# Differential attention in a two-block model: the order of the query-block rounds within each head

## The chip, the cores and the metric

One core of one Trainium2 chip. The metric is the device time of one execution in microseconds (us). The whole program (two model blocks) is timed, and the change touches one stage of it, the attention.

## The reference

512 tokens, model width 1024. A first block (convolutions, spatial gating, an expert lookup) is followed by a second one: a state-space mixer, a feed-forward part, then differential attention and another feed-forward part. The attention is what matters here:

```python
def block(args):                                   # one block of 128 queries
    idx, qc = args
    rel = k_pos[None, :] - q_pos[:, None]
    bias = rel_bias[t5_causal_bucket(rel)]...
    s = jnp.einsum("bqhcd,bkhcd->bhcqk", qc, k) * scale      # c: two halves of a head
    s = jnp.where(rel <= 0, s + bias, NEG_INF)
    pm = jax.nn.softmax(s, axis=-1)
    attn = pm[:, :, 0] - lam * pm[:, :, 1]
    return jnp.einsum("bhqk,bkhe->bqhe", attn, v)
...
o = rms_norm(o, subln) * (1.0 - lam_init)
return o.reshape(...) @ w_o
```

There are 8 heads and 4 blocks of 128 queries. A block sees only the keys up to its own end, so block 0 has 128 keys, block 1 has 256, block 2 has 384 and block 3 has 512.

## The kernel before

Each engine has its own instruction stream, written out by hand; semaphores tie them together. The attention works through `QUERIES = HEADS * NR = 24` rounds, three for each head. `ROUNDS` (L351) says which query blocks a round holds: blocks 0 and 1 together (128 and 256 columns side by side in a bank), then block 2 (384 columns), then block 3 (512 columns). Below they are called the **narrow pair**, the **third** and the **widest**. `members(v)` lists the blocks of round v; `exps_until(v)` gives the count of exponentials that are finished when round v is, which other engines wait for.

A round v passes through these steps:

- TensorE, `scores2(v)` (L1118): the products of queries and keys for both halves, into two of four score banks (`score_bank`). It waits for the exponentials of round v-2, which free the banks.
- VectorE, `highest(v)`: per row the extreme of the scores, over the far keys a plain reduction (L2595), over the last 256 keys together with the bias (L2598). The narrow pair needs no L2595, but twice the L2598.
- ScalarE, `exps(v)` (L1734): the exponentials with their sums, per block one for each half.
- VectorE, `share(v)` (L2608, L2610) and `blend(v)` (L2618): the ratio of the two softmaxes' sums, and their weighted difference.
- TensorE, `turn(v)` (L1131): transposes of that difference, one for each 128 keys.
- ScalarE, `turned(v)` (L1744): copies them to where the next product reads them.

When all rounds of a head are through, TensorE does `values(h)` (L1143), the product with the values. ScalarE takes it out in `head_out(h)` (L1751, L1754). `head_stat`, `spread` (L1155, L1170), `batch_root` (L1760, two table loads beside it), `batch_inverse` (L2624) and `head_norm` (L2631) normalise finished heads in between; POOL makes the low half of a finished head in `norm_low` (L2722), and splits weights for the output product (L2675, L2677 before the rounds, L2750, L2752 beside them).

The loops are staggered by hand. VectorE does `highest(u+1)`, now and then `head_norm`, then `share(u)`, `blend(u)`. TensorE does `scores2(u+2)`, `turn(u-1)`, and after it, by the place j of round u-1 in its head, `values(h-1)` (j = 0) or `head_stat(h-1)` (j = 1). ScalarE does `exps(u+1)`, `turned(u-1)`, and `head_out(h-1)` if round u-1 has j = 0. `scores2(0)` and `scores2(1)` are issued earlier, inside the products that make the second half of the values (L1088); ScalarE copies those values out (L1715) between `exps(1)` and `exps(2)`, and `scores2(3)` waits for these copies. `values(4)` and others wait for `on_ready`, the signal of `head_norm` (`SPREADS_BEFORE`), since they share a bank.

Of the kernel before, what the change touches and what calls it, by code (L numbers as in the profile page):

```python
# [17 lines left out]
NT = SEQ // P  # L18
# [54 lines left out]
def build(nc, A, first=0, last=99):  # L73
# [24 lines left out]
    with ctx:  # L98
# [28 lines left out]
        def view(arena, at, *shape):  # L127
            n = int(np.prod(shape))
            v = arena[:, at:at + n]
            if len(shape) == 2:  # L130
                v = v.rearrange("p (a b) -> p a b", b=shape[1])
            elif len(shape) == 3:
                v = v.rearrange("p (a b c) -> p a b c", b=shape[1], c=shape[2])
            elif len(shape) == 4:
                v = v.rearrange("p (a b c d) -> p a b c d", b=shape[1], c=shape[2], d=shape[3])
            return v
# [211 lines left out]
        qgain = R[:, 14008:14009]  # L348
        ROWS16 = 4 * NT
        sel = view(R, 14016, ROWS16, ROWS16)  # L350
        ROUNDS = ((0, 1), (2,), (3,))  # L351
        NR = len(ROUNDS)
        BATCHES = ((0, 1, 2), (3, 4), (5, 6, 7))
        BATCH = [g for g in range(3) for h in BATCHES[g]]
# [34 lines left out]
        def members(v):  # L389

            at = 0
            for part, qt in enumerate(ROUNDS[v % NR]):
                w = (qt + 1) * P
# [2 lines left out]

        def exps_until(v):

            return 2 * (v // NR * NT + ROUNDS[v % NR][-1]) + 2

        def score_bank(u):

# [133 lines left out]
        def _(pe):  # L536
# [505 lines left out]
            if stage("attn"):  # L1042
# [59 lines left out]
                def scores2(v):  # L1102

                    h = v // NR
                    if v % NR == 0:
                        pe.wait_ge(kq_ready, HEADS + h + 1)
                    if v == 0:
                        pe.wait_ge(evac_done, used(TILE0["w_v"] + 3))
                    if v == 1:
                        pe.wait_ge(gq_sqrt, 2 * HEADS)  # L1110
                    if v >= 2:
                        pe.wait_ge(exp_done, exps_until(v - 2))
                    if v == 3:
                        pe.wait_ge(evac_done, used(TILE0["w_v"] + 7))
                    for part, u, qt, at, w in members(v):
                        for c in range(2):
                            rows, out = slice(c * HD, (c + 1) * HD), banks[score_bank(v) + c]
                            mm = pe.matmul(out[:, at:at + w], KQ[rows, HEADS + h, qt * P:(qt + 1) * P], KQ[rows, h, 0:w],  # L1118
                                           start=True, stop=True)
                    mm.then_inc(at_sc, 1)  # L1120

                def turn(v):

                    pe.wait_ge(cb_done, v + 1)
                    if v == 0:
                        pe.wait_ge(exp_done, exps_until(1))
                    if v >= 2:
                        pe.wait_ge(tr_ev, exps_until(v - 2) // 2)
                    for part, u, qt, at, w in members(v):
                        for kt in range(qt + 1):  # L1130
                            mm = pe.transpose(banks[4 + v % 2][:, at + kt * P:at + (kt + 1) * P],  # L1131
                                              att[:, v % 2, at + kt * P:at + (kt + 1) * P], ident)
                    mm.then_inc(tr_mm, 1)
# [657 lines left out]
        def _(ve):  # L1791
# [764 lines left out]
            if stage("attn"):  # L2556
# [47 lines left out]
                def share(v):  # L2604
                    n, u = len(ROUNDS[v % NR]), v // NR * NT + ROUNDS[v % NR][0]
                    r = ratio[:, v % 2, 0:n]
                    ve.wait_ge(exp_done, exps_until(v))
                    ve.reciprocal(r, sums[:, u:u + n, 1])  # L2608
                    ve.drain()
                    ve.scalar_tensor_tensor(r, r, nlam, sums[:, u:u + n, 0], ALU.mult, ALU.mult)  # L2610
                    ve.drain()
# [338 lines left out]
```

## Time and profile before

| | |
|---|---|
| median of 3 runs | 2934.83 us (2932.98 to 2935.81) |
| profiled execution: its own time | 2934.74 us |
| profiled execution: span of the trace | 2932.9 us |
| busy over the span: TensorE, VectorE, POOL, ScalarE | 2622.4, 1937.4, 1673.5, 826.2 us |
| attention rounds, first L2598 to last L2618 | 2391.65 to 2472.23 us |
| in the stretch 2384 to 2480 us: VectorE, TensorE, ScalarE busy | 74.88, 79.22, 64.22 us of 96 |
| mean granted TensorE clock in that stretch | 0.91 of full |

The profile gives busy times by engine and line, what ended each idle time, and the instructions in order of time. A stretch can be queried alone, which is what a change of one stage asks for: the rounds take 80.6 of 2932.9 us.

### The profile page before, as it was taken

The numbers are of one execution on the slowest core, as the hardware profiler recorded it, in microseconds if no ns is written. First come the engines' busy times: TensorE is split into PE (matmuls) and PEld (weight loads), VectorE is DVE, ScalarE is ACT, GpSimd is POOL, SyncE is SP. The second block draws the span as 40 slices with busy tenths as digits, with TensorE's granted clock in tenths as the row PEclk, the third lists the DMA queues.
The fourth block names the chain that finished last, engine by engine and source line by source line (L and its number), as shares of the span: only waits on it lengthen the run. The fifth ranks groups of instructions, "written<-read, shape, count | busy, mean of one in ns | idle before, by whom it ended". The sixth has DMA issues, their size and how long they took to land.

```text
span 2932.9 us, 32353 instructions
## 1 busy us (share of the span) xinstructions
PE 2622.4 (89%) x9810; PEld 1211.8 (41%) x9810; DVE 1937.4 (66%) x3944; ACT 826.2 (28%) x1800; POOL 1673.5 (57%) x1024
## 2 busy tenths in 40 slices
PE   7989888887888888887878999999999998999999
PEld 3454333333333333333333684444444445444444
DVE  7947777777777777777877683666336596566523
ACT  2422222222222222222234461222112246222101
POOL 5544444444444444444535877777776651677776
PEclk9999999999999999999999979999999999999999
DMA  4259999999999999999972322333322320233332
GB/s 138 71 192 421 421 421 417 411 420 417 413 416 409 417 410 421 411 411 419 414 312 69 105 74 88 94 101 105 117 95 86 117 72 8 79 100 102 120 98 82
DMA packets 133100, 696.18 MB, mean 237 GB/s; under 512 B 29867, under 2 KB 31180, under 8 KB 67052
## 3 DMA queue, kind: packets, MB, share of 16 engines
q0 software_dynamic: 73728, 536.90, 44.4%
q1 hardware_dynamic: 59244, 157.74, 16.6%
q8 instruction: 60, 0.98, 0.1%
q14 instruction: 68, 0.56, 0.1%
HBM read 686.72 MB, written 7.86 MB: 237 GB/s over the span
## 4 chain that ended last, share of the span: by engine, by line
PE 33%; DMA 26%; POOLq 16%; DVE 12%; issue 7%; ACT 3%; DVEq 2%; POOL 2%; ACTq 0%; SPq 0%
DMA R<-expert_uv_dram,idx 25%; PE bank L573 20%; PE bank L787 8%; POOLq L2678 8%; POOLq L2676 7%; DVE R L2106 3%; DVE Z L2128 1%; POOL R L2703 1%; DVE xt L2391 1%; ACT Z L1390 1%; DVE R L1851 1%; PE bank L1143 1%; PE bank L956 1%; DVE ci L2052 0%; DVE R L2118 0%
## 5 line engine op out<-in xcount | busy, mean ns | idle before, releaser
L787 PE MATMUL bank<-R,Z 128*128 128x512 f32 x2048 | 972.5, 619 | 227.2 <-ACT Z L1390 222.3
L2703 POOL DMA_INDIRECT R<-expert_uv_dram,idx x512 | 595.2, 1162 | 722.7 <-PE bank L787 673.2
L573 PE MATMUL bank<-R 128*128 128x512 f16 (+1 forms) x3936 | 865.6, 381 | 8.9 <-DVE R L1835 6.1
L2106 DVE SCALAR_TENSOR_TENSOR R<-R 128x1024 f32<-128x1024 f32 x512 | 622.9, 1222 | 198.2 <-DMA R<-expert_uv_dram,idx 196.8
L787 PEld LDWEIGHTS bank<-R,Z 128*128 128x128 f32 x2048 | 382.4, 195 | 800.4 <-issue 419.9
L2675 POOL TENSOR_TENSOR R<-wring,beat 128x1024 f16<-128x1024 f32 (+2 forms) x219 | 447.1, 2041 | 396.7 <-PE bank L573 349.2
L573 PEld LDWEIGHTS bank<-R 128*128 128x128 f16 (+1 forms) x3936 | 382.6, 98 | 490.3 <-issue 26.6
L2677 POOL TENSOR_TENSOR R<-wring,R 128x1024 bf16<-128x1024 f32 (+2 forms) x219 | 510.1, 2329 | 31.8 <-issue 0.3
L1390 ACT ACTIVATE Z<-consts,R 128x128 f32<-128x128 f32 x512 | 177.7, 394 | 322.1 <-DVE R L2118 320.0
L573 PE MATMUL bank<-Z,R 128*128 128x512 f16 x1104 | 239.9, 379 | 1.5 <-POOLq L2678 1.5
L1383 ACT ACTIVATE R<-R 128x2 f32<-128x2 f32 x256 | 52.1, 203 | 607.3 <-DVEq L2108 607.0
L573 PEld LDWEIGHTS bank<-Z,R 128*128 128x128 f16 x1104 | 107.8, 98 | 132.2 <-POOLq L2678 2.5
L1508 ACT ACTIVATE R<-bank,cols 128x512 f32<-128x512 f32 x88 | 68.4, 777 | 324.8 <-DVE bank L2361 324.8
L1879 DVE TENSOR_TENSOR hT<-hT,bank 128x512 f32<-128x512 f32 x32 | 22.0, 688 | 204.1 <-PE bank L573 204.1
L2361 DVE TENSOR_TENSOR bank<-bank,sq 128x512 f32<-128x512 f32 x88 | 61.2, 695 | 129.6 <-PE bank L573 124.7
L573 PE MATMUL bank<-aT,R 128*128 128x512 f16 (+1 forms) x576 | 130.7, 388 | 5.1 <-DVE aT L2170 4.4
L1267 ACT ACTIVATE bank<-hT 128x512 f32<-128x512 f32 x56 | 33.5, 598 | 246.9 <-DVE hT L1879 216.5
L2118 DVE SCALAR_TENSOR_TENSOR R<-R 128x2 f32<-128x2 f32 x256 | 56.2, 220 | 58.8 <-ACT R L1383 47.4
L573 PEld LDWEIGHTS bank<-aT,R 128*128 128x128 f16 (+1 forms) x576 | 56.9, 99 | 76.8 <-issue 8.2
L1851 DVE SCALAR_TENSOR_TENSOR R<-hT,cols,R 128x512 bf16<-128x512 f32 x48 | 82.5, 1732 | 0.7
L2367 DVE SCALAR_TENSOR_TENSOR R<-bank,cols,R 128x511 f32<-128x511 f32 x88 | 65.6, 745 | 16.7 <-issue 16.7
L806 PE MATMUL bank<-aT,Z 128*128 128x512 f32 x144 | 73.6, 592 | 0.0
(365 smaller groups left out, 2513.2 us busy)
## 6 DMA issues: line engine op xcount, KB each, us to landing
wring<-up_dram SPq DMA_DIRECT2D x88, 512.0 KB, 3.5
wring<-down_dram SPq DMA_DIRECT2D x32, 704.0 KB, 4.1
wring<-ple_dram SPq DMA_DIRECT2D x16, 640.0 KB, 3.9
wring<-w_in_dram SPq DMA_DIRECT2D x18, 512.0 KB, 3.5
R<-expert_uv_dram,idx POOLq DMA_INDIRECT x512, 12.2
wring<-glu_dram SPq DMA_DIRECT2D x16, 512.0 KB, 4.1
Z<-w_q_dram SPq DMA_DIRECT2D x11, 512.0 KB, 7.8
wring<-ple_a_dram SPq DMA_DIRECT2D x8, 640.0 KB, 5.9
```

The lines of the kernel that those rows point to most:

```text
L573: mm = pe.matmul(bank[:, :], low(w) if i else w, low(v) if j else v, start=(start and c == 0 and p == 0), stop=(stop and c == n - 1 and p ...
L787: mm = pe.matmul(banks[2 * par + c][:, :], diag[:, k % 4, :], pairs[:, slot, 1, c * SEQ:(c + 1) * SEQ], start=(k == 0), stop=(k == TOPK - 1))
L806: mm = pe.matmul(banks[6 + half][:, :], w[:, k * P:(k + 1) * P], aT[:, k, :], start=(k == 0), stop=(k == KT - 1))
L1390: ac.activation(diag[:, k % 4, :], ident, ACT.Copy, scale=actg[:, par, k:k + 1])\
L1508: ac.activation(conv[:, u, gv, :], banks[(2 * u + gv) % NBANK][:, :], ACT.Identity, bias=cols[:, bass.ds(at + b, 1)], scale=cols[:, bass.d ...
L1851: ve.scalar_tensor_tensor(low(parts[:, k, 1, :]), hT[:, k, :], col(gain, k), parts[:, k, 0, :], ALU.mult, ALU.subtract).then_inc(gn_ready, 1)
L2106: dot = ve.scalar_tensor_tensor(pairs[:, slot, 0, :], pairs[:, slot, 0, :], 1.0, ntok[:, T, :], ALU.mult, ALU.mult, accum_out=act[:, par, ...
L2675: po.tensor_tensor(wsp[:, slot, 0, 0:w], src, one.broadcast_to([P, w]), ALU.mult)
L2676: po.drain()
L2677: po.tensor_tensor(low(wsp[:, slot, 1, 0:w]), src, wsp[:, slot, 0, 0:w], ALU.subtract)
L2678: po.drain().then_inc(split_done, 1)
L2703: po.indirect_dma_start(pairs[:, slot, :, :].rearrange("p a b -> p (a b)"), None, A["expert_uv"], bass.IndirectOffsetOnAxis(idx[:, n % 2, ...
```

## The change

Within each head the widest round comes first, then the third, then the narrow pair. `exps_until` counts the exponentials over the rounds as they now stand.

```diff
-        ROUNDS = ((0, 1), (2,), (3,))
+        ROUNDS = ((3,), (2,), (0, 1))
...
         def exps_until(v):
 
-            return 2 * (v // NR * NT + ROUNDS[v % NR][-1]) + 2
+            return 2 * (v // NR * NT + sum(len(r) for r in ROUNDS[:v % NR + 1]))
```

No instruction is added or taken away. POOL's and SyncE's streams stay as they are. Below, `bank<-Z 128x512 x2` at L1118 are the scores of the widest round, 128x384 those of the third, 128x128 and 128x256 those of the narrow pair.

TensorE at the start of the attention rounds, where the value products (L1088) end; the difference, `-` before and `+` now:

```order
 L1088 MATMUL bank<-R 128x512 x12
+L1118 MATMUL bank<-Z 128x512 x2
+L1118 MATMUL bank<-Z 128x384 x2
+L1088 MATMUL bank<-R 128x512 x24
 L1118 MATMUL bank<-Z 128x128 x2
 L1118 MATMUL bank<-Z 128x256 x2
+L1118 MATMUL bank<-Z 128x512 x2
+L1131 MATMUL bank<-consts,R 128x128 x4
 L1118 MATMUL bank<-Z 128x384 x2
-L1088 MATMUL bank<-R 128x512 x24
-L1118 MATMUL bank<-Z 128x512 x2
```

The two score groups inside the value products are now the widest and the third, and the one that waits for the value copies (the second group behind the 24 products) is the widest instead of the narrow pair.

TensorE in the second head, around its first `values`, before:

```order
L1118 MATMUL bank<-Z 128x128 x2
L1118 MATMUL bank<-Z 128x256 x2
L1131 MATMUL bank<-consts,R 128x128 x3
L1143 MATMUL bank<-R 128x512
L1143 MATMUL bank<-R 128x384
L1143 MATMUL bank<-R 128x256
L1143 MATMUL bank<-R 128x128
L1118 MATMUL bank<-Z 128x384 x2
```

and now:

```order
L1118 MATMUL bank<-Z 128x512 x2
L1131 MATMUL bank<-consts,R 128x128 x4
L1143 MATMUL bank<-R 128x512
L1143 MATMUL bank<-R 128x384
L1143 MATMUL bank<-R 128x256
L1143 MATMUL bank<-R 128x128
L1118 MATMUL bank<-Z 128x384 x2
```

`values` and what stands behind it are where they were; ahead of it now stand the scores and the four transposes of a widest round, not those of a narrow pair.

VectorE at the end of the rounds, before:

```order
L2631 SCALAR_TENSOR_TENSOR xt<-aT,sub,bank 128x512
L2608 RECIPROCAL R<-R 128x1
L2610 SCALAR_TENSOR_TENSOR R<-R 128x1
L2618 SCALAR_TENSOR_TENSOR R<-Z,R 128x384
L2608 RECIPROCAL R<-R 128x1
L2610 SCALAR_TENSOR_TENSOR R<-R 128x1
L2618 SCALAR_TENSOR_TENSOR R<-Z,R 128x512
L2624 RECIPROCAL rstd<-rstd 16x128
```

and now:

```order
L2631 SCALAR_TENSOR_TENSOR xt<-aT,sub,bank 128x512
L2608 RECIPROCAL R<-R 128x1
L2610 SCALAR_TENSOR_TENSOR R<-R 128x1
L2618 SCALAR_TENSOR_TENSOR R<-Z,R 128x384
L2608 RECIPROCAL R<-R 128x2
L2610 SCALAR_TENSOR_TENSOR R<-R 128x2
L2618 SCALAR_TENSOR_TENSOR R<-Z,R 128x128
L2618 SCALAR_TENSOR_TENSOR R<-Z,R 128x256
L2624 RECIPROCAL rstd<-rstd 16x128
```

The last difference that VectorE forms is that of the narrow pair, in two instructions, instead of the widest block's in one.

## Rows read from the trace of the kernel before

**Rows 1.** The page, part 1: busy time, share of the span, instructions of each engine.

```profile
PE 2622.4 (89%) x9810; PEld 1211.8 (41%) x9810; DVE 1937.4 (66%) x3944; ACT 826.2 (28%) x1800; POOL 1673.5 (57%) x1024
```

**Rows 2.** Waits, 2384 to 2480 us: who waited for whom, us in total, times, longest.

```profile
DVE xt L2631 <- PE bank L1170: 2.4, 3, 1.3
DVE R L2595 <- PE bank L1118: 1.2, 1, 1.2
...
DVE R L2608 <- ACT Z L1734: 0.2, 1, 0.2
```

**Rows 3.** Timeline of VectorE, one head: start us, us, engine, line, operation.

```profile
2417.40 0.29 DVE L2598 CUSTOM_DVE_ANT_0 bank<-bank,R 128x128 f32<-128x128 f32 x1
...
2418.88 0.16 DVE L2608 RECIPROCAL R<-R 128x1 f32<-128x1 f32 x1
...
2420.08 0.42 DVE L2595 TENSOR_REDUCE R<-bank 128x2 f32<-128x256 f32 x1
...
2421.69 0.17 DVE L2608 RECIPROCAL R<-R 128x2 f32<-128x2 f32 x1
...
2422.89 0.68 DVE L2595 TENSOR_REDUCE R<-bank 128x2 f32<-128x512 f32 x1
...
2424.76 0.17 DVE L2608 RECIPROCAL R<-R 128x1 f32<-128x1 f32 x1
...
2425.83 0.29 DVE L2598 CUSTOM_DVE_ANT_0 bank<-bank,R 128x128 f32<-128x128 f32 x1
```

**Rows 4.** Timeline of ScalarE in the same head.

```profile
2416.28 0.69 ACT L1734 ACTIVATE Z<-bank,R 128x512 f32<-128x512 f32 x1 [1.37 <-DVEq L2602]
...
2417.53 0.20 ACT L1734 ACTIVATION_READ_ACCUMULATOR Z<-bank,R 128x1 f32 x1
...
2419.14 0.37 ACT L1734 ACTIVATE Z<-bank,R 128x128 f32<-128x128 f32 x1
...
2420.62 0.23 ACT L1734 ACTIVATION_READ_ACCUMULATOR Z<-bank,R 128x1 f32 x1
```

**Rows 5.** Timeline of TensorE in the same head.

```profile
2420.91 1.13 PE L1118 MATMUL bank<-Z 64*128 64x512 f32 x4 [0.48 <-ACT Z L1734]
2421.97 0.66 PE L1131 MATMUL bank<-consts,R 128*128 128x128 f32 x4
2423.02 0.93 PE L1118 MATMUL bank<-Z 64*128 64x128 f32 x8 [0.39 <-ACT Z L1734]
...
2424.26 2.32 PE L1143 MATMUL bank<-R 128*128 128x512 f32 x8
```

**Rows 6.** Timeline of all engines at the start of the rounds.

```profile
2389.05 2.38 POOL L2677 TENSOR_TENSOR R<-wring,R 128x1024 bf16<-128x1024 f32 x1
2389.63 1.82 DVE L2582 SCALAR_TENSOR_TENSOR R<-R 128x1 f32<-128x1 f32 x1 [0.18 <-issue]
...
2395.83 2.42 ACT L1715 ACTIVATE R<-bank,R 128x512 f32<-128x512 f32 x4
...
2398.40 1.65 PE L1118 MATMUL bank<-Z 64*128 64x128 f32 x8 [1.46 <-ACT R L1715]
...
2403.29 1.93 PE L1118 MATMUL bank<-Z 64*128 64x512 f32 x4
```

**Rows 7.** Timeline of VectorE, the three places where it waits in the rounds.

```profile
2440.94 0.75 DVE L2631 SCALAR_TENSOR_TENSOR xt<-aT,sub,bank 128x512 f32<-128x512 f32 x1 [0.92 <-PE bank L1170]
...
2450.88 0.42 DVE L2595 TENSOR_REDUCE R<-bank 128x2 f32<-128x256 f32 x1 [1.20 <-PE bank L1118]
...
2453.63 0.75 DVE L2631 SCALAR_TENSOR_TENSOR xt<-aT,sub,bank 128x512 f32<-128x512 f32 x1 [1.25 <-PE bank L1170]
```

**Rows 8.** Timeline of TensorE, an idle time without and two idle times with slow matmuls behind.

```profile
2433.95 0.93 PE L1118 MATMUL bank<-Z 64*128 64x128 f32 x8 [2.88 <-ACT Z L1734]
...
2445.90 4.09 PE L1143 MATMUL bank<-R 128*128 128x512 f32 x8 [0.94 <-DVEq L2632]
...
2469.94 4.02 PE L1143 MATMUL bank<-R 128*128 128x512 f32 x8 [1.87 <-DVEq L2632]
```

**Rows 9.** Busy time by stretch: stretch, length, PE, PEld, DVE, ACT, POOL, PEclk, DMA share, GB/s.

```profile
2445.90:2449.40 3.50, 3.50 (x6) 1.83 (x7) 3.08 (x14) 0.91 (x4) 0.00 (x0) 0.51 0.00 0
```

## The prediction, made before the changed kernel was run

> **What bounds the kernel now.** Begin with the busy times of the whole page [rows 1]: TensorE is busy 89% of the span, but that is a mean over sixteen stages, and the change touches only 80.6 us of the 2932.9. So the stage is read alone. Its list of waits [rows 2] shows who holds up whom: VectorE waits for TensorE's bank spreads 2.4 us in all, once 1.2 us for scores, and for exponentials 0.2 us. That is 3.8 us in 80.6; the other engines wait for VectorE far longer. The timeline of one head on VectorE [rows 3] shows why. From the start of one round's maxima to the start of the next step there are 1.48 us for the narrow pair (2417.40 to 2418.88), 1.61 for the third (2420.08 to 2421.69), 1.87 for the widest (2422.89 to 2424.76). Share and blend take 1.20 for the widest (2418.88 to 2420.08), 1.20 for the narrow pair (2421.69 to 2422.89) and 1.07 for the third (2424.76 to 2425.83). The six add up to 8.43 us, and that is just the head's period (2417.40 to 2425.83). VectorE never stands still in such a head: **it is the bound**, and a reordering doesn't change a sum. What can change are the start, the end, and the places where VectorE waits for others.
>
> **The change, part by part.**
>
> *Steady heads: nothing.* The cycle becomes widest, third, narrow pair. It stays at 8.43 us as long as the other two engines deliver in time. ScalarE: its exponentials take 1.45 us for the widest (2416.28 to 2417.73) and 1.71 for the narrow pair (2419.14 to 2420.85) [rows 4]. Between them lie the copy of the transposes and the two instructions that take a head out, 2.86 - 1.45 = 1.41 us. Before, the narrow exponentials ended at 2420.85 and their share began at 2421.69 [rows 3, 4]: 0.84 us of slack. Now the head's exit stands behind the narrow pair's exponentials and ahead of the widest's. Count from the end of the narrow maxima: ScalarE is free at 1.71 + 1.41 = 3.12; the widest maxima are ready at 1.07 + 1.87 = 2.94; the exponentials then end at 3.12 + 1.45 = 4.57, and their share is due at 2.94 + 1.20 + 1.61 = 5.75. That leaves 1.2 us, from which the values product may take some: ahead of it TensorE now has widest scores (1.13 us instead of 0.93) and four transposes (0.66 us, so at most 0.17 more than three; I take 0.12) [rows 5], 0.32 us in all. I keep 0.8 us of slack. TensorE: before, the widest scores ended at 2422.04 and were wanted at 2422.89 [rows 3, 5], 0.85 us; now they follow the exponentials of the third of the head before, and are wanted only after maxima of the narrow pair and a share, so the slack is no smaller. Nothing is added per head. At the two places where ScalarE loads tables for a square root, the exponentials ahead of the loads are now the widest's, 0.26 us shorter.
>
> *Start: +0.8 us.* Three small delays follow each other. The two score groups inside the value products are widest and third instead of narrow and third: +0.20 us on TensorE [rows 5]. POOL's weight split follows TensorE there, and VectorE's L2582 (1.82 us for one column) ends at 2391.45, just as POOL's L2677 ends at 2391.43 [rows 6]; so the first maxima start 0.20 later. Their widest form lasts 1.87 - 1.48 = 0.39 longer, but the second exponentials start only 0.32 later, since they waited 0.07 for the narrow ones before and now wait for their own maxima alone, and so do the value copies of 2.42 us behind them [rows 6]. The scores that wait for these copies are now the widest at the low clock, 1.93 instead of 1.65 us: +0.28 [rows 6]. Together 0.20 + 0.32 + 0.28 = 0.80. All of it is on the path, since VectorE takes these scores about as they come.
>
> *First bank spread (2440.94, VectorE waits 0.92) [rows 7]: +0.3 us.* VectorE arrives 0.39 later in its count of work, because the widest maxima precede. TensorE's chain to the spread starts from exponentials behind ScalarE's table loads: they come 0.39 + 0.2 later (0.39 the maxima; and 0.2 because ScalarE, free 2.86 - 2.55 = 0.3 us after the narrow maxima were ready [rows 3, 4], now waits for the longer TensorE chain as well), less 0.26; then the wider scores and the fourth transpose, +0.32. That is 0.65, against 0.39: 0.26 more waiting, rounded to 0.3.
>
> *Scores behind values of the fifth head (2450.88, waits 1.20) and the spread behind them (2453.63, waits 1.25) [rows 7]: -0.4 us.* The values product starts when VectorE has normed a head; all three maxima and the same shares lie before that point in either order, so it does not move. But VectorE now has widest maxima between this point and its wait, not after it: 0.39 us of work moves into the wait. The second wait keeps its length, as both sides hang on the same product.
>
> *End: -0.15 us.* The last round has three transposes instead of four (-0.12) and two short copies instead of a long one (a few hundredths).
>
> DMA issues, POOL's and SyncE's queues are not moved. Sum: 0.80 + 0.3 - 0.4 - 0.15 = **+0.55 us**. Behind the rounds TensorE runs the output product at once, so it passes on in full. Against the profiled execution's own time that is 2934.74 + 0.55 = 2935.3; the median of the runs lies 0.1 higher, so I say **2935.4 us**.
>
> **The clock, a term of the range.** Two values products took 4.09 and 4.02 us instead of 2.32 [rows 5, 8]; in the first the granted clock was 0.51 [rows 9], the lower of TensorE's two levels (1.2 GHz of 2.4). Ahead of them the engine had stood idle 0.94 and 1.87 us. Yet after 2.88 us idle at 2433.95 the scores still ran in 0.93 us [rows 8], so idle time alone does not tell where the clock falls. My sum leaves both slow products where they are, since the same instructions stand ahead of them. If neither were slow, 2 x 1.75 = 3.5 us go, and the start loses its 0.8: 0.55 - 4.3 = -3.8. If two more products are slow, +3.5: +4.1. The Trainium skill (TensorE: Matmul & The Clock Gate, What's actually happening) says that an engine left idle falls to the lower level and that the monitor runs freely, whatever the kernel does. By that rule the slow products could fall anywhere, and the time would move by those amounts without any cause in the order.
>
> **The rivals.**
>
> 1. *The low clock falls on other products* (0.25): 2931.0 to 2939.0, as worked out. For it: the idle times around the products shift by some tenths. Against: the waits that cause them stay.
> 2. *VectorE and POOL collide elsewhere* (0.09). L2582 shows such a collision: 1.82 us for one column. A POOL split lasts up to 2.38 us [rows 6], so one more or one less moves the time by at most that: 2933 to 2937.7. The Trainium skill (SBUF — State Buffer) calls the shared port pair an exclusive lock for a whole instruction; the end at 2391.45 beside POOL's 2391.43 agrees.
> 3. *Slower: the head's exit holds up the widest exponentials* (0.07). ScalarE runs in order, and behind the head's exit, which waits for the values product, now stand the exponentials that VectorE needs next, behind a longer TensorE chain. It decides once the product ends over 0.8 us later than I have it. At the low clock a product takes 1.75 us more; 1.75 - 0.8 = 0.95 us in each of 7 heads is 6.6, with the sum 2935.4 + 6.6 = 2942. For it: ScalarE's start is already late by some tenths. Against: the same exit stood ahead of the narrow exponentials with 0.84 us of slack, and no head showed a wait.
> 4. *Faster: the narrow pair last takes the waits away* (0.04). All three waits of rows 7 vanish (3.4), the last slow product runs at full clock (1.7) and L2582 no longer meets POOL (at most 1.8): 2934.8 - 6.9 = 2928. Against: two of the waits hang on a product that the change doesn't move.
>
> **How the numbers follow.** My forecast has the remaining 0.55: 2935.4, with the spread of the runs 2933.9 to 2936.9. The range takes in rivals 1 and 2: 2931.0 to 2939.0, and leaves out about 0.15 at both sides. 0.2% is 5.9 us, about what a measurement of this kernel can tell from no change; only rival 3 passes it upwards and rival 4 downwards. So faster 0.04, same 0.89, slower 0.07.
>
> **What would show it.** Right: a steady head on VectorE still 8.4 us; the scores behind the value copies widest, 1.9 us long and 0.5 us later than 2398.40, and VectorE taking them at once; no long wait of L2608 for L1734; the wait of L2595 for L1118 near 0.8 instead of 1.2; the last blend within 1 us of its place. Wrong: L2608 waiting for L1734 in every head (rival 3), a period other than 8.4 us, or a different number of values products at 4 us.

## The result, and the profile after

| | before | changed |
|---|---|---|
| median of 7 runs | 2935.06 us (2932.98 to 2936.39) | 2942.59 us (2940.93 to 2953.89) |
| profiled execution: its own time, span | 2934.74, 2932.9 us | 2943.72, 2941.9 us |
| stage, from the start of L2582 to that of the first L1879 | 107.85 us | 114.84 us |

The ratio is 1.0028, with a 95% interval of 1.0019 to 1.0037: the change makes the kernel slower by 7.5 us in the medians, by 5.6 to 10.9 with the interval. The forecast was 2935.4, with a range up to 2939.0; the time lies above it.

The busy times of the whole page hardly moved (compare [rows 1]):

```profile
PE 2625.0 (89%) x9810; PEld 1213.3 (41%) x9810; DVE 1941.4 (66%) x3944; ACT 825.9 (28%) x1800; POOL 1675.9 (57%) x1024
```

VectorE's 4.0 us more for the same 3944 instructions is the first hint: some of them have become longer. To find where the time went I measure the stage between two events that both kernels have, the last VectorE instruction ahead of the rounds (L2582) and the first addition of the output product to the stream (L1879). The timeline of VectorE, before (the end of the stage) and then changed (both ends):

```profile
2497.48 0.69 DVE L1879 TENSOR_TENSOR hT<-hT,bank 128x512 f32<-128x512 f32 x1 [3.70 <-PE bank L573]
```

```profile
2391.64 1.82 DVE L2582 SCALAR_TENSOR_TENSOR R<-R 128x1 f32<-128x1 f32 x1 [0.18 <-issue]
...
2506.48 0.69 DVE L1879 TENSOR_TENSOR hT<-hT,bank 128x512 f32<-128x512 f32 x1 [3.75 <-PE bank L573]
```

Before, L2582 began at 2389.63 [rows 6], so the stage took 107.85 us, and it takes 114.84 now. The other 2.0 us of the difference of the spans lie ahead of L2582, where no instruction was moved; a second trace of the kernel before, below, has its L2582 at 2391.64 as well.

The waits of the stretch 2384 to 2490 us of the changed kernel, as in [rows 2]:

```profile
DVE R L2595 <- PE bank L1118: 4.2, 3, 1.6
```

There is no wait of VectorE for exponentials among the long ones: rival 3 is not what happened. But VectorE now waits three times for scores, not once. A steady head, on VectorE's timeline, as in [rows 3]:

```profile
2422.28 0.68 DVE L2595 TENSOR_REDUCE R<-bank 128x2 f32<-128x512 f32 x1
...
2424.14 0.17 DVE L2608 RECIPROCAL R<-R 128x2 f32<-128x2 f32 x1
...
2425.34 0.42 DVE L2595 TENSOR_REDUCE R<-bank 128x2 f32<-128x256 f32 x1
...
2426.95 0.16 DVE L2608 RECIPROCAL R<-R 128x1 f32<-128x1 f32 x1
...
2428.15 0.29 DVE L2598 CUSTOM_DVE_ANT_0 bank<-bank,R 128x128 f32<-128x128 f32 x1
...
2429.63 0.16 DVE L2608 RECIPROCAL R<-R 128x1 f32<-128x1 f32 x1
...
2430.70 0.68 DVE L2595 TENSOR_REDUCE R<-bank 128x2 f32<-128x512 f32 x1
```

Maxima 1.86, 1.61 and 1.48 us, share and blend 1.20, 1.20 and 1.07: the head takes 8.42 us (2422.28 to 2430.70), as before. So the steady cycle is not it. VectorE's groups by shape, first of the kernel before and then of the changed one (line, engine, operation, shapes, count; busy us, mean ns; idle before), 2384 to 2500 us, show what is:

```profile
L2618 DVE SCALAR_TENSOR_TENSOR R<-Z,R 128x384 f32<-128x384 f32 x8 | 4.9, 618 | 0.6
L2618 DVE SCALAR_TENSOR_TENSOR R<-Z,R 128x256 f32<-128x256 f32 x8 | 3.8, 479 | 0.0
```

```profile
L2618 DVE SCALAR_TENSOR_TENSOR R<-Z,R 128x256 f32<-128x256 f32 x8 | 7.6, 947 | 0.0
...
L2618 DVE SCALAR_TENSOR_TENSOR R<-Z,R 128x384 f32<-128x384 f32 x8 | 5.8, 726 | 0.6
```

The second blend of the narrow pair (256 columns) costs 3.8 us more in the stage. The third's 0.9 us more is one blend of 1.48 us at 2465.27, held up by POOL's L2722 (2465.18 to 2466.33); before, the same L2722 held up a L2610 at 2458.94, 1.09 us instead of 0.22, so that is no loss of the change. The timeline of all engines around one of the two places (the other is at 2433.43) gives the mechanism; first ScalarE's and POOL's rows, then VectorE's:

```profile
2411.33 0.48 ACT L1734 ACTIVATE Z<-bank,R 128x256 f32<-128x256 f32 x1
...
2412.05 1.89 POOL L2750 TENSOR_TENSOR Z<-wring,beat 128x1024 f16<-128x1024 f32 x1 [13.89 <-ACT Z L1734]
...
2414.08 2.28 POOL L2752 TENSOR_TENSOR Z<-wring,Z 128x1024 bf16<-128x1024 f32 x1
```

```profile
2413.42 0.53 DVE L2610 SCALAR_TENSOR_TENSOR R<-R 128x2 f32<-128x2 f32 x1
...
2414.03 2.62 DVE L2618 SCALAR_TENSOR_TENSOR R<-Z,R 128x128 f32<-128x128 f32 x2
```

POOL's weight split is released by the exponentials of a head's last round, which is now the narrow pair. Its first half (L2750) ends at 2413.94 and holds L2610 up until then. VectorE's first narrow blend starts at 2414.03, just ahead of POOL's second half (L2752, 2414.08). Between the two narrow blends POOL gets its turn, and the second blend waits for the whole of it: the pair takes 2.62 us instead of 0.75, +1.87. Twice, that is 3.7 us.

The kernel before had the same meeting at less cost. POOL's rows there, then VectorE's:

```profile
2408.99 1.89 POOL L2750 TENSOR_TENSOR Z<-wring,beat 128x1024 f16<-128x1024 f32 x1 [12.85 <-ACT Z L1734]
...
2411.02 2.69 POOL L2752 TENSOR_TENSOR Z<-wring,Z 128x1024 bf16<-128x1024 f32 x1
```

```profile
2410.24 0.66 DVE L2610 SCALAR_TENSOR_TENSOR R<-R 128x1 f32<-128x1 f32 x1
...
2410.97 0.75 DVE L2618 SCALAR_TENSOR_TENSOR R<-Z,R 128x512 f32<-128x512 f32 x1
```

L2610 is held up by the first half, 0.66 us instead of 0.22. The widest round's blend is one instruction: it starts 0.05 us ahead of the second half, takes its usual 0.75 us, and it is POOL that waits (2.69 us; the same operation took 2.13 before the rounds, at 2394.01).

Three rows of VectorE answer to those of [rows 7], the scores behind `values(3)`, the bank spread after them, and the spread behind the second table load:

```profile
2446.95 0.42 DVE L2595 TENSOR_REDUCE R<-bank 128x2 f32<-128x256 f32 x1 [1.31 <-PE bank L1118]
...
2449.49 0.75 DVE L2631 SCALAR_TENSOR_TENSOR xt<-aT,sub,bank 128x512 f32<-128x512 f32 x1 [1.04 <-PE bank L1170]
...
2473.95 0.75 DVE L2631 SCALAR_TENSOR_TENSOR xt<-aT,sub,bank 128x512 f32<-128x512 f32 x1 [1.03 <-PE bank L1170]
```

And TensorE's rows, as in [rows 6, 8]; a row of L1143 with fewer than x8 is only the first part of a values product:

```profile
2400.76 2.08 PE L1118 MATMUL bank<-Z 64*128 64x512 f32 x4 [2.66 <-ACT R L1715]
...
2439.26 2.08 PE L1118 MATMUL bank<-Z 64*128 64x512 f32 x4 [2.61 <-ACT Z L1734]
...
2442.17 3.45 PE L1143 MATMUL bank<-R 128*128 128x512 f32 x5
...
2464.30 2.08 PE L1118 MATMUL bank<-Z 64*128 64x512 f32 x4 [3.00 <-ACT Z L1734]
...
2467.21 3.21 PE L1143 MATMUL bank<-R 128*128 128x512 f32 x7
...
2478.51 3.33 PE L1143 MATMUL bank<-R 128*128 128x512 f32 x4 [0.97 <-DVEq L2632]
```

The widest scores behind the table loads take 2.08 us instead of 1.13, and the values products behind them 3.89 and 3.32. The mean granted clock was 0.58 from 2437.4 to 2444.2 and 0.60 from 2464.3 to 2470.5. The low clock lies on the products of heads 3, 5 and 6 (4.55 us) now; before it lay on heads 4 and 6.

**Theories.** One: collision between POOL's split and the narrow pair's two blends, 3.7 us, plus the low clock behind the table loads, some 3 us, plus the later start, about 1 us. Rival: the reversed cycle itself costs time in the queues of TensorE and ScalarE, and the long instructions are only where it shows.

### The profile page after: what moved, and what is told of

It reads as the page before. It is cut to its first block, busy times and chain, and to the rows that moved or that the text cites. A ratio compares the mean times of both kernels' runs of the same rounds, so it can differ in the third digit from the quotient of the medians.

```text
span 2941.9 us, 32353 instructions
## 1 busy us (share of the span) xinstructions
PE 2625.0 (89%) x9810; PEld 1213.3 (41%) x9810; DVE 1941.4 (66%) x3944; ACT 825.9 (28%) x1800; POOL 1675.9 (57%) x1024
## 4 chain that ended last, share of the span: by engine, by line
PE 32%; DMA 26%; POOLq 15%; DVE 13%; issue 8%; ACT 3%; DVEq 2%; POOL 2%; ACTq 0%; SPq 0%
DMA R<-expert_uv_dram,idx 25%; PE bank L573 20%; POOLq L2678 8%; PE bank L787 8%; POOLq L2676 7%; DVE R L2106 3%; POOL R L2703 1%; DVE Z L2128 1%; DVE xt L2391 1%; ACT Z L1390 1%; DVE R L1851 1%; PE bank L1143 1%; DVE R L2499 1%; DVE ci L2052 0%; DVE R L2118 0%
## 5 line engine op out<-in xcount | busy, mean ns | idle before, releaser
L573 PE MATMUL bank<-R 128*128 128x512 f16 (+1 forms) x3936 | 864.9, 381 | 9.6 <-DVE R L1835 6.4
L573 PEld LDWEIGHTS bank<-R 128*128 128x128 f16 (+1 forms) x3936 | 382.3, 98 | 490.2 <-issue 25.3
L573 PE MATMUL bank<-Z,R 128*128 128x512 f16 x1104 | 239.9, 379 | 1.5 <-POOLq L2678 1.5
L573 PEld LDWEIGHTS bank<-Z,R 128*128 128x128 f16 x1104 | 107.8, 98 | 132.2 <-POOLq L2678 2.5
L1879 DVE TENSOR_TENSOR hT<-hT,bank 128x512 f32<-128x512 f32 x32 | 22.0, 688 | 203.3 <-PE bank L573 203.3
L573 PE MATMUL bank<-aT,R 128*128 128x512 f16 (+1 forms) x576 | 130.1, 387 | 5.8 <-DVE aT L2170 4.5
L573 PEld LDWEIGHTS bank<-aT,R 128*128 128x128 f16 (+1 forms) x576 | 56.8, 99 | 77.1 <-issue 7.9
```

The lines of the kernel that those rows point to most:

```text
L573: mm = pe.matmul(bank[:, :], low(w) if i else w, low(v) if j else v, start=(start and c == 0 and p == 0), stop=(stop and c == n - 1 and p ...
```

## The experiments

Medians are set beside the kernel before on the same chip; the ratio and the difference of the two medians can disagree by up to 1.4 us. The stage is from each kernel's trace, one execution. "Slow products" are values products of more than 2.6 us, by their head, 0 to 7.

| kernel | median, us | before, us | ratio, 95% interval | stage, us | slow products |
|---|---|---|---|---|---|
| splits held back, changed order | 2939.13 | 2936.81 | 1.0010 (1.0001 to 1.0019) | 110.76 | 3, 5, 6 |
| old order, splits on the narrow pair | 2940.03 | 2936.81 | 1.0006 (0.9997 to 1.0015) | 111.46 | 3, 5 |
| third, widest, narrow | 2943.28 | 2936.81 | 1.0024 (1.0013 to 1.0035) | 114.12 | 1, 3, 4, 5, 6 |
| narrow, widest, third | 2939.14 | 2936.81 | 1.0009 (1.0000 to 1.0018) | 110.81 | 3, 5, 6 |
| changed order, extra products | 2938.41 | 2937.39 | 1.0003 (0.9993 to 1.0012) | 110.22 | 1, 6 |
| old order, extra products | 2933.02 | 2937.39 | 0.9988 (0.9979 to 0.9997) | 104.59 | none |
| changed order, all three mended | 2932.89 | 2937.39 | 0.9984 (0.9975 to 0.9993) | 104.15 | none |
| before again | 2936.84 | 2937.39 | one run | 107.95 | 4, 6 |
| changed again | 2944.03 | 2936.80 | 1.0037 (1.0023 to 1.0050) | 114.06 | 1, 3, 6 |
| mended, scores released early | 2932.99 | 2936.80 | 0.9986 (0.9977 to 0.9995) | 104.16 | none |
| old order, the same edits | 2935.62 | 2936.80 | 0.9995 (0.9986 to 1.0004) | 106.91 | none |

**Splits held back.** POOL waits for the head's last blend as well:

```diff
                             po.wait_ge(exp_done, 2 * NT * (i - 1) * 2)
+                            po.wait_ge(cb_done, NR * (i - 1) * 2)
```

> The changed kernel, with POOL's two weight splits beside the rounds (L2750, L2752) held back until the head's last blend is through, instead of its last exponentials. Theory 1 (collision): in the changed kernel the second half of a split starts between the two blends of the narrow pair and holds the second one up, 1.87 us twice, 3.7 us of the change's 7 to 8. Then both L2618 of 2.62 us are gone from the trace, POOL costs VectorE at most 0.5 us a split, and the time is 3 to 4 us below the changed kernel: near +4 us against the kernel before. Theory 2 (order and clock alone): the time stays at +7 to +8, since slow matmuls behind the table loads and the later start make all of it.

The same place on VectorE and POOL in this run:

```profile
2414.56 0.75 DVE L2618 SCALAR_TENSOR_TENSOR R<-Z,R 128x128 f32<-128x128 f32 x2
```

```profile
2415.48 1.90 POOL L2751 TENSOR_TENSOR Z<-wring,beat 128x1024 f16<-128x1024 f32 x1 [16.49 <-ACT Z L1734]
```

POOL starts when both narrow blends (0.75 us together) are through. No blend pair of 2.6 us is left, the stage is 4.1 us below the first trace of the changed kernel and 3.3 below the second, and the median is 2.3 us above before instead of 7.5. The slow products are those of the first trace (3, 5, 6), and two blend pairs (3.7 us) and two L2610 of 0.32 instead of 0.53 us (0.4) account for the 4.1. Theory 1 holds for this part.

**Old order, splits on the narrow pair.** In the kernel before, the splits wait for four more exponentials, those of the next head's narrow pair:

```diff
-                            po.wait_ge(exp_done, 2 * NT * (i - 1) * 2)
+                            po.wait_ge(exp_done, 2 * NT * (i - 1) * 2 + 4)
```

> The kernel before in its old order, with only the two weight splits beside the rounds moved: they wait for the next head's narrow exponentials too, so that they meet the narrow pair's share. Theory 1 (collision): POOL's first half blocks L2610, its second half slips between the two narrow blends; L2618 of about 2.6 us appears twice, and the kernel becomes 3.5 to 5 us slower than before though the order of rounds is the old one. Theory 2: POOL's place is of no account, 0 within 1.5 us.

```profile
2411.86 1.89 POOL L2750 TENSOR_TENSOR Z<-wring,beat 128x1024 f16<-128x1024 f32 x1 [16.07 <-ACT Z L1734]
...
2413.89 2.28 POOL L2752 TENSOR_TENSOR Z<-wring,Z 128x1024 bf16<-128x1024 f32 x1
```

```profile
2412.71 1.06 DVE L2610 SCALAR_TENSOR_TENSOR R<-R 128x2 f32<-128x2 f32 x1
...
2413.84 2.61 DVE L2618 SCALAR_TENSOR_TENSOR R<-Z,R 128x128 f32<-128x128 f32 x2
```

With the order untouched the same picture appears: L2610 held up until the first half ends, the narrow pair 2.61 us, twice. The stage grows by 3.6 us, the median by 3.2, below the 3.5 to 5 that I expected, and the ratio's 1.0006 is only 1.8 us, with no change inside its interval; the trace is the stronger evidence. The slow products moved as well (3 and 5 instead of 4 and 6), so the size of the growth is not the collision's alone. What the rows show is that the collision needs the narrow pair behind the split's release, and not the new order.

**Third, widest, narrow** and **narrow, widest, third** are one line each:

```diff
-        ROUNDS = ((3,), (2,), (0, 1))
+        ROUNDS = ((2,), (3,), (0, 1))
```

```diff
-        ROUNDS = ((3,), (2,), (0, 1))
+        ROUNDS = ((0, 1), (3,), (2,))
```

> The changed kernel with the rounds third, widest, narrow pair: the narrow pair is still last in its head, but the cyclic order (narrow, third, widest) is that of the kernel before. Theory 1 (collision, because the split is released by the narrow exponentials and so meets the narrow blends): slow as well, L2618 above 2 us twice, +4 us or more. Rival (the reversed cycle costs time in TensorE and ScalarE): back to within 2 us of the kernel before.

> The changed kernel with the rounds narrow pair, widest, third: the cycle is the reversed one of the change, but the third is last, with a single blend. Theory 1 (collision): no L2618 above 1.5 us at the splits, and the time is near the kernel before, +0 to +3 us with the clock's part. Rival (the reversed cycle): +6 us or more, as the change.

The first keeps the old cycle, with the narrow pair last:

```profile
2415.74 2.62 DVE L2618 SCALAR_TENSOR_TENSOR R<-Z,R 128x128 f32<-128x128 f32 x2
```

The second has the reversed cycle, with the third last; its blend is a single instruction, and POOL's second half comes behind it:

```profile
2410.23 0.62 DVE L2618 SCALAR_TENSOR_TENSOR R<-Z,R 128x384 f32<-128x384 f32 x1
```

+6.5 us against +2.3: for the collision it matters who is last in a head, not in which direction the rounds go. That settles the rival. The 3.0 us by which the second one's stage still exceeds that of before are not the split's: slow are the products of heads 3, 5 and 6 there, as in the first trace of the change.

**Extra products.** Four unused products of 256 columns stand ahead of the scores behind each table load; for the old order and the mended kernel, three more ahead of the values products of heads 4 and 6:

```diff
                 for u in range(QUERIES + 1):
+                    if u in (13, 19):
+                        if u == 19:
+                            pe.wait_ge(on_ready, 3)
+                        for _ in range(4):
+                            pe.matmul(banks[6][:, 0:2 * P], ident, consts[:, 0:2 * P], start=True, stop=True)
...
+                        for _ in range(3 if h in (4, 6) else 0):
+                            pe.matmul(banks[4][:, 0:2 * P], ident, consts[:, 0:2 * P], start=True, stop=True)
```

> The changed kernel with four extra products of 256 columns on TensorE ahead of the scores that wait behind each of the two square-root table loads; their results are not used. Theory (clock): in the changed kernel these scores and the values product after them ran at the low clock (2.08, 3.89 and 2.08, 3.32 us), and VectorE waited 1.31 and 1.60 us for the scores behind them. With TensorE occupied the clock stays up, both products take 2.3 us, both waits of L2595 fall below 0.3 us, and the stage from L2582 to the first L1879 is 2.5 to 3 us shorter than the changed kernel's 114.8. If the low clock comes regardless of what TensorE does, nothing changes or it is up to 2 us longer. The collisions (L2618 of 2.62 us, twice) stay in either case.

```profile
2435.98 1.89 PE L1182 MATMUL bank<-consts 128*128 128x256 f32 x8
...
2439.03 1.13 PE L1118 MATMUL bank<-Z 64*128 64x512 f32 x4 [1.16 <-ACT Z L1739]
...
2440.58 2.32 PE L1143 MATMUL bank<-R 128*128 128x512 f32 x8
```

The scores behind the first table load take 1.13 us again and the values product 2.32; so does the second pair, and both waits of VectorE for these scores are gone. The stage falls by 4.6 us against the first trace and 3.8 against the second, more than the 2.5 to 3 I expected: counted from L2582, the norm behind the first table load comes 1.7 us earlier than in the first trace, the one behind the second 4.1. The blend pairs of 2.62 us stay, and two products that have no extra ones ahead of them are slow, heads 1 and 6.

> The kernel before with the same extra products, and with three more ahead of each of the two values products that wait for a norm (heads 4 and 6, 4.09 and 4.02 us in the trace of before). Theory (clock): no values product above 2.6 us, the wait of 1.20 us for scores and most of the 1.25 us for a spread gone, the last product 1.7 us shorter: stage 104 to 106 us instead of 107.9, time 2 to 4 us below the kernel before. Rival: the low clock comes at fixed times whatever TensorE does, no gain.

```profile
2445.61 1.46 PE L1142 MATMUL bank<-consts 128*128 128x256 f32 x6
...
2446.91 2.32 PE L1145 MATMUL bank<-R 128*128 128x512 f32 x8
```

All eight values products run at full clock, and the stage is 3.3 us shorter than the kernel before. So the low clock had cost the old order as well, at other places. (Behind the rounds it stayed low here too; see the next run.)

> The changed order with the splits held back until the head's last blend (as in the earlier run, stage 110.8 us) and all the extra products. Both causes taken away, only the later start should remain: stage 107 to 109 us, time within 1.5 us of the kernel before (and 1 to 4 us above the old order with the same extra products). If more than 3 us above the kernel before remain, a third cause is missing.

104.15 us: better than the 107 to 109 expected. For one part, I had measured from the old order's 107.9, which still held its own slow products. The other part lies behind the rounds, in the output product (L573), of which I had expected nothing. The old order with the extra products, then this kernel:

```profile
2488.28 4.77 PE L573 MATMUL bank<-R,Z 128*128 128x512 f16 x15
```

```profile
2500.53 3.41 PE L573 MATMUL bank<-R,Z 128*128 128x512 f16 x15
```

The granted clock over these rows is 0.71 in the first and 1.00 in the second. From the first norm behind the rounds to the first L1879 it takes 8.71 us in the old order with extra products, as in the kernel before, and 7.07 here, though no edit aims at that place. So the 0.4 us between the two stages (104.15 against 104.59) do not compare the orders. Up to that norm the old order takes 95.88 us from L2582 and this kernel 97.08: the reversed order is 1.2 us behind, although its splits no longer hold up any L2610 by more than 0.1 us, and those of the old order still do, by 0.44 twice. (The trace is that of the kernel's slowest execution, 2943.17 us; the time was lost ahead of the stage, whose L2582 begins at 2401.77.)

**Both kernels once more**, unedited.

> The kernel before once more, for its trace: whether the low clock falls on the same products as in the first trace (values of heads 4 and 6). If the clock depends on the order of the work alone, the same two; if it depends on where the kernel happens to start, others, also those behind the table loads, and the stage takes 107 to 111 us.

> The changed kernel once more, unchanged, beside the other two on one chip. If collision and clock are properties of the order, its trace repeats the first: stage (L2582 to the first L1879) 114.8 us within 0.3, two L2618 of 2.62 us, slow products of heads 3, 5 and 6, and the time is 6 to 8 us above the kernel before. If the slow products move, the clock's part is chance.

The kernel before repeats itself to 0.1 us, with the same slow products. The changed one is at 114.06, not 114.8 within 0.3: the two pairs of 2.62 us are there, but the slow products are those of heads 1, 3 and 6 (the rows show their first parts; 3.43 and 3.32 us in all for heads 1 and 3):

```profile
2418.86 3.21 PE L1143 MATMUL bank<-R 128*128 128x512 f32 x6
...
2439.57 3.21 PE L1143 MATMUL bank<-R 128*128 128x512 f32 x7
```

The collision is a property of the order, then. Where the slow products fall is not wholly one: head 1 was hit instead of head 5 (2.59 us now), and by the test that I had set myself that part is chance. The stage differed by 0.8 us. Two traces of each kernel can't say more about how much of the clock's part is chance.

**Scores released early.** The fourth round's scores wait for the two copies that free their own banks:

```diff
                     if v == 3:
-                        pe.wait_ge(evac_done, used(TILE0["w_v"] + 7))
+                        pe.wait_ge(evac_done, used(TILE0["w_v"] + 5))
```

> The changed order with the splits held back, the extra products, and the scores of the fourth round waiting for the two value copies that free their own banks, not for all four. Theory: the start term of the change is the wait of L2595 for these scores, 1.34 us; two copies of 0.6 us less ahead of them shorten it by 1.2, stage 103.0 us (104.15 before this edit). If the stage stays at 104, the start was not on the path.

VectorE's wait for these scores in the mended kernel, and with the edit:

```profile
2413.00 0.69 DVE L2602 TENSOR_REDUCE R<-bank 128x2 f32<-128x512 f32 x1 [1.34 <-PE bank L1118]
```

```profile
2401.67 0.69 DVE L2602 TENSOR_REDUCE R<-bank 128x2 f32<-128x512 f32 x1 [0.18 <-PE bank L1118]
```

The wait falls from 1.34 to 0.18 us, and the head start of 1.15 us lasts up to the last norm within the rounds (78.01 us after L2582 instead of 79.16). Yet the stage stays at 104.16: ahead of the last late values product the extra products themselves ran slowly, 2.53 us for 1.46, and stood in its way:

```profile
2469.33 2.53 PE L1142 MATMUL bank<-consts 128*128 128x256 f32 x6
...
2471.70 2.32 PE L1145 MATMUL bank<-R 128*128 128x512 f32 x8
```

At the first norm behind the rounds the two kernels are level (97.09 and 97.08 us). The start is on the path of the rounds, then, but what it gives was lost again at the end, to the remedy and not to the order.

> The old order with the same three edits. There the fourth round's scores were taken only 0.15 us late, so their earlier release is worth at most 0.2 us, and the held-back splits save at most the 0.44 us twice that L2610 lost: stage 103.5 to 104.6 us (104.59 with the extra products alone). If the order of rounds has no cost of its own in steady heads, this and the changed order with the same edits lie within 1 us of each other, both 3 to 6 us below the kernel before.

This one missed, by 2.3 us, and its own trace says why:

```profile
2412.14 1.71 DVE L2617 SCALAR_TENSOR_TENSOR R<-R 128x2 f32<-128x2 f32 x1
...
2430.87 2.62 DVE L2625 SCALAR_TENSOR_TENSOR R<-Z,R 128x128 f32<-128x128 f32 x2
```

In the old order the held-back splits are released by the widest blend, and the next share is the narrow pair's: one L2610 (here L2617) of 1.71 us, one blend pair of 2.62. The remedy for one order made the collision in the other, which is the mechanism once more. Of the 2.75 us between this stage and that of the changed order with the same edits, 1.1 arise up to the first norm behind the rounds (98.15 against 97.09), and 1.7 behind it, where the output product ran at the low clock here as well.

## Why the prediction was wrong

It forecast +0.55 us, and the stage grew by 6.99. By its own steps, counted from L2582:

- *Steady heads: nothing.* Right: 8.42 us, and no wait for exponentials. But the step looked at two engines only. It said that POOL's queue is not moved, and did not ask what releases POOL's splits: they wait for the exponentials of a head's last round, so they moved from the widest to the narrow pair. The trace of before showed both meetings, in two L2610 of 0.66 us. Two pairs of 2.62 instead of 0.75 us are +3.7; two L2610 that are 0.13 shorter than before give back 0.25. This is **the step that failed**, and half of the loss.
- *Rival 2, the collision,* had the right mechanism and a chance of only 0.09. Its price, "one more or one less moves the time by at most that", meant one collision and either sign; there are two splits beside the rounds, and both fall on the pair. What the price missed is the gap between two blends, through which POOL's second half slips.
- *Start: +0.8 us.* About right. The fourth round's maxima begin 11.23 us after L2582 (2402.87) instead of 10.46 (2400.09): +0.77, where 0.60 of my sum lay behind L2582. The scores took 2.08 us, not 1.93.
- *First bank spread: +0.3 us.* The norm at 2449.49 comes 6.54 us later than before; less 0.77 and 3.5, that is +2.3. Most of it is the clock, since the chain to the spread ran through scores of 2.08 and a values product of 3.89 us: with the extra products the same norm comes 1.74 us earlier. The other 0.6 stays with them. 0.39 of it are the widest maxima, which the step counted as VectorE's work but left out of its 0.3. An idle time of 0.48 us ahead of a L2608 at 2421.21 also lies before this norm; the old order has none there, and no view names its cause.
- *Scores behind the values of head 4: -0.4 us.* It was -2.2. About 1.6 of that is the product, which ran at full clock (the extra products gave the old order 1.57 up to the same norm); the remaining -0.6 is near the forecast. By the third norm (2460.00) the delay was 4.36 us.
- *Not in the sum at all:* the second table load, where the same happened as at the first. The norm at 2473.95 is 6.94 us late, another +2.6. With the extra products only 0.2 of it is left, so 2.4 are the clock's.
- *End: -0.15 us.* +0.05.

The sum is 0.77 + 3.5 + 2.3 - 2.2 + 2.6 + 0.05 = 7.0. The clock's part of it is 1.7 - 1.6 + 2.4 = +2.5, an estimate from the runs with extra products and inside the 3.5 that the range allowed for two more slow products. The collision's is +3.5, and +1.0 is left for the order itself, where the steps behind L2582 had +0.35. But "my sum leaves both slow products where they are, since the same instructions stand ahead of them" was wrong. That was the second step that failed: heads 3, 5 and 6 and two groups of scores were slow, not heads 4 and 6. The range could hold either cause alone. It could not hold both.

The Trainium skill (SBUF — State Buffer, Who interferes with whom) calls the port pair that VectorE and GpSimd (POOL) share an exclusive lock: a VectorE instruction with two SBUF inputs contends with a GpSimd instruction that reads SBUF. The traces agree: wherever L2752's turn came between the two narrow blends, in both traces of the changed kernel and in four of the others, the second blend waited for the whole of it, and the pair took 2.61 or 2.62 us. I had named this rule only beside a small rival; applied to the release of the splits it would have given the main term.

What stays open is which stretch falls to the lower of TensorE's two levels. In both traces of the kernel before, the scores after 2.88 us of idle time ran at full clock; with the splits moved, in the same order and behind the same idle time, they ran low:

```profile
2435.96 0.93 PE L1118 MATMUL bank<-Z 64*128 64x128 f32 x8 [2.88 <-ACT Z L1734]
```

```profile
2435.87 1.65 PE L1118 MATMUL bank<-Z 64*128 64x128 f32 x8 [2.88 <-ACT Z L1734]
...
2438.15 3.62 PE L1143 MATMUL bank<-R 128*128 128x512 f32 x5
```

(The row of L1143 is the first part of a product of 4.33 us.) The runs with extra products show that the scores and products right behind a filled idle time ran at full clock. They don't show what decides on one that is not filled, and once the extra products were themselves slow.

## What to carry to other kernels

When a table of numbers reorders rounds, list every wait on another engine that counts those rounds, those of "unmoved" queues too, and ask what will be running when each is now released. Where VectorE and POOL work beside each other, a step made of two short instructions is dearer than one long one, since POOL can take its turn between them: 2.62 us instead of 0.75. One instruction can still be held up at its start, as the blend of 1.48 us shows. And in this kernel TensorE's idle times of 1 to 3 us were worth filling where a product on the path follows: fourteen spare products took 3.3 us off the old order's stage. In the changed order such products once ran slowly themselves and cost about 1 us. The old order with them (2933.02 us) and the changed one with splits held back and extra products (2932.89) both lie 4 us below the kernel before on their chip (2937.39), 0.1 to 0.2% with intervals that just exclude no change; the first needs fewer edits.

## What the runs showed that was not expected

- The kernel before, by itself, lost 3.3 us to the low clock. Its 4.09 and 4.02 us products stood in [rows 8], and I took them as given instead of as something to remove. Another 1.6 us hung on the clock at the output product, which ran at full clock only in the two changed-order kernels with held-back splits and extra products; why there is open.
- A reversed cycle costs nothing in a steady head, 8.42 us. But it isn't free over the rounds: with collision and slow values products gone it was 1.2 us behind the old order at the first norm behind them (97.08 against 95.88), and only the faster output product made the stages look alike (104.15 and 104.59 us).
- A remedy depends on the order: holding the splits back saved 3.3 to 4.1 us in the changed order, while with it (and the earlier release of scores) the old order's stage was 106.91 instead of 104.59 us.
